# Choosing and gathering the first two turns of a mixture of experts in the mixing stage, and splitting the weights during the first expert product

## The chip, the core and the metric

One core of a Trainium2 chip runs the whole program. The metric is device microseconds of one execution. TensorE is written PE (its weight loads PEld), VectorE DVE, ScalarE ACT, GpSimd POOL, and SyncE SP.

## What is computed

Two layers over 1024 tokens of 1024 features: a token mixer (windowed attention in layer 0, a Fourier mixing in layer 1), then a mixture of 64 experts of which every token takes 8, plus one shared expert. The part that matters here is the second, cut to its core:

```python
def moe_ffn(tok, ...):
    scores = sigmoid(tok @ router_w)
    top_e = top 8 experts of the 4 best of 8 groups, by scores + bias
    wts = scores[top_e] / sum(scores[top_e]) * 2.5
    # the rows of every expert are gathered in blocks of 128
    for each block of an expert e, with rows `rows` and weights `wb`:
        xb = x_pad[rows]
        hb = silu(xb @ w_gate[e]) * (xb @ w_up[e])
        y[rows] += (hb @ w_down[e]) * wb[:, None]
    return y + (silu(tok @ s_gate) * (tok @ s_up)) @ s_down
```

## The kernel before

`moe` runs two blocks for each layer, `mix` and `experts`. A block ends when all five engines have come to its end. Then the stage's semaphores are cleared and all engines meet once more (lines 234 and 235), so that nothing of the next block starts before the last engine of the block is done.

`mix` multiplies by the output matrix, normalises, runs the shared expert in eight tiles of 128 tokens (`gate_up`, `turn_h`, `down`, with ACT's `store` and SP's write of the result to DRAM), and routes. At its end PE turns the table of places and weights (L1307, L1313), and DVE copies the places to SBUF (L1141). DVE makes a one-hot matrix for turn 0 in the 16-bit tile `hot` (L1143), which says for every slot of the turn which token stands there. It casts the weights to 16 bits into `moving[..., 3]` (L1146). PE multiplies the one-hot with three columns of `moving` (L1319), then runs `down(7)`, the last tile of the shared expert. DVE turns the product into row numbers `idx` (L1149 to L1151) and POOL gathers these rows of `u_scratch` into `xg[:, 0]` with an indirect DMA (L1022). After that DVE makes the second and third 16-bit part of the weights (L1153 to L1156). A weight in fp32 is the sum of three 16-bit parts.

`experts` works in turns of 128 rows. There are 71 in each layer, and a turn has one or two experts. In layer 0 turn 0 has the expert in ring slot 0, turn 1 that in slot 1, turn 2 those in slots 2 and 3. In layer 1 turn 1 already has two, slots 1 and 2, and turn 2 slots 2 and 3. Per turn: a one-hot (`onehot`, DVE, L1449), a product with all six columns of `moving` into `psI` (`index`, PE, L1638), the row numbers and the weights from it (`indices`, DVE, L1464 to L1472), the gather (POOL, L1415), the turned rows (`turn_rows`, PE, L1656, copied by ACT L1602 and DVE `rows` L1479), the first product (`gate_up`, PE, L1668, into `psG`), the activation (ACT L1607, DVE `hidden` L1484 to L1488), the turned result (PE L1690, ACT L1612), the second product (`down`, PE, L1702, into `psD`), the weighing (DVE L1517) and the scattered addition to `y_scratch` (POOL, L1426).

The order on each engine is written out by hand. `xg`, `hot`, `psG`, `hid` and `yo` have two buffers, so that the gather of turn 2 can be issued only when the rows of turn 0 have been turned. SP loads the experts' weights into a ring of four slots, 3 MB each (L2222 gate and up, L2225 down). Slot 0 is loaded in `mix` (L1003 to L1005). Slots 1 to 3 are loaded at the start of `experts`, after a wait for the last write of the shared expert's result (L1373). Each later load waits until the turns that used its slot are done. `table`, `overflow` and the loops with `_over` serve experts with more rows than planned, and the change does not touch them.

The beginning of PE's program in `experts` is this:

```python
                        pe.sem_inc(d_mm, 1)
                        index(0, 0)
                        index(1, 1)
                        turn_rows(0, 0, 16)
                        index(2, 0)
                        gate_up(0, 0)
                        turn_rows(1, 1, 16)
                        index(3, 1)
```

## Time and profile before

| | us |
|---|---|
| median of three runs | 2992.59 |
| lowest and highest | 2986.41, 2995.37 |
| the profiled execution | 2990.77 |
| its span, from first to last instruction | 2989.0 |
| between the two, outside the span | 1.8 |

The mean clock that TensorE was granted is 0.979 of full speed. The expert stages run from 797 to 1674 us (layer 0) and from 2050 to about 2940 us (layer 1). A row of the time line gives the start, the duration, the engine, the line, and in brackets how long the engine stood idle before it and what released it. PE instructions of one kind that follow one another are merged. Each fp32 product shows as two instructions.

### The profile page before, as it was taken

The page shows a single profiled execution, that of the slowest core. Times are in us where ns is not written, and L with a number is a line of the kernel's source. Part 1 is how long each engine was busy: PE and PEld are TensorE (multiplying, and loading weights), DVE is VectorE, ACT ScalarE, POOL GpSimd, SP SyncE. Part 2 cuts the span into 40 slices and gives each one's busy share as a digit, 9 for nine tenths or more (in the row PEclk, how much of TensorE's full clock was granted, in tenths as well). Part 3 has the DMA queues.
Part 4 walks back from the last instruction along what each step waited for, and adds up shares of the span by engine and source line. Part 5 has one row for each costly group of instructions (what it writes and reads, how often), then busy time and mean ns, then how long its engine had stood idle before and what let it go on. Part 6 is the DMA issues. An engine that isn't in the chain of part 4 may idle for free. (4 is left out here: it accounts for less than half of the span.)

```text
span 2989.0 us, 40809 instructions
## 1 busy us (share of the span) xinstructions
PE 2821.1 (94%) x15284; PEld 1368.5 (46%) x15287; DVE 1753.3 (59%) x3359; ACT 509.5 (17%) x1060; POOL 532.5 (18%) x404
## 2 busy tenths in 40 slices
PE   8998999999899999999999598997999999999994
PEld 3444666544444444444444264543444444444442
DVE  4994555466656555555555455665565555555555
ACT  1113555201110111111111240011110111111112
POOL 0000000111022222222222211101222222222212
PEclk9999999999999999999999899998999999999997
DMA  9777200201599999999999622017999999998996
GB/s 365 258 271 215 78 15 8 77 29 42 206 338 331 310 299 321 328 339 329 353 306 321 208 99 83 29 50 282 306 296 332 296 366 320 320 345 275 311 325 197
DMA packets 147086, 715.70 MB, mean 239 GB/s; under 512 B 16702, under 2 KB 21950, under 8 KB 94665
## 3 DMA queue, kind: packets, MB, share of 16 engines
q1 hardware_dynamic: 104252, 556.83, 48.6%
q0 software_dynamic: 42336, 154.16, 20.8%
q8 instruction: 124, 2.03, 0.3%
q10 hardware_dynamic: 304, 2.11, 0.2%
q14 instruction: 70, 0.57, 0.1%
HBM read 598.18 MB, written 114.84 MB: 239 GB/s over the span
## 5 line engine op out<-in xcount | busy, mean ns | idle before, releaser
L1668 PE MATMUL exG<-ring,xT 128*32 128x512 f32 (+2 forms) x2352 | 683.4, 596 | 5.2 <-DMA ring<-in_exp_w_up_dram 3.7
L1479 DVE COPY xT<-exX 128x512 f32<-128x512 f32 x146 | 101.0, 692 | 680.5 <-PE exX L1656 680.2
L1668 PEld LDWEIGHTS exG<-ring,xT 128*32 128x32 f32 (+2 forms) x2352 | 240.0, 141 | 348.0 <-issue 343.4
L1702 PE MATMUL exD<-ring,ex_hT 128*32 128x512 f32 (+2 forms) x1176 | 353.2, 603 | 1.7 <-DVE w_fnet L1517 0.8
L1612 ACT ACTIVATE ex_hT<-exH 128x256 f32<-128x256 f32 x144 | 55.2, 383 | 1454.5 <-PE exH L1690 1454.5
L1485 DVE RECIPROCAL ex_e<-ex_e 128x256 f32<-128x256 f32 x142 | 249.0, 1753 | 5.0
L1668 PE MATMUL exG<-oT,xT 128*32 128x512 f32 (+2 forms) x592 | 192.5, 597 | 1.3 <-DVE xT L1479 1.3
L1426 POOL DMA_INDIRECT y_scratch<-w_fnet,idx_out x72 | 136.1, 1891 | 299.1 <-DMA y_scratch<-w_fnet,idx_out 156.3
L1426 POOL DMA_INDIRECT y_scratch<-w_o,idx_out x72 | 132.8, 1844 | 306.3 <-DMA y_scratch<-w_o,idx_out 166.8
L1449 DVE TENSOR_TENSOR mod<-place,slots 128x1024 bf16<-128x1024 f32 (+3 forms) x196 | 174.1, 912 | 8.1 <-PEq L235 7.4
L1668 PE MATMUL exG<-w_fnet,xT 128*32 128x512 f32 (+2 forms) x608 | 172.2, 599 | 4.8 <-DMA ring<-in_exp_w_up_dram 4.8
L1702 PEld LDWEIGHTS exD<-ring,ex_hT 128*32 128x32 f32 (+2 forms) x1176 | 115.0, 140 | 126.4 <-issue 125.4
L753 DVE TENSOR_REDUCE mx<-pair 128x2 f32<-128x1280 f32 x64 | 95.5, 1492 | 125.5 <-PE pair L865 125.5
L1668 PE MATMUL exG<-w_o,xT 128*32 128x512 f32 (+2 forms) x464 | 148.2, 593 | 0.7 <-DVE xT L1479 0.7
L287 POOL TENSOR_TENSOR rstd<-var,halves 128x1 f32<-128x1 f32 x42 | 62.9, 1498 | 465.8 <-DVE var L273 465.8
L1415 POOL DMA_INDIRECT fT<-u_scratch,idx x72 | 71.2, 989 | 378.6 <-DVEq L1474 378.6
L1415 POOL DMA_INDIRECT oT<-u_scratch,idx x72 | 71.2, 989 | 366.6 <-DVEq L1474 356.2
L1668 PE MATMUL exG<-fT,xT 128*32 128x512 f32 (+2 forms) x432 | 121.5, 597 | 0.9 <-DVE xT L1479 0.9
L1223 PE MATMUL mixY<-w_fnet,fT 128*128 128x512 f32 x256 | 113.4, 601 | 6.0 <-PEq L235 4.6
L1223 PE MATMUL mixY<-w_o,oT 128*128 128x512 f32 x256 | 111.7, 594 | 3.1 <-PEq L235 1.7
L1244 PE MATMUL mixG<-sh_gate_up,u2T 128*128 128x512 f32 x256 | 112.6, 593 | 0.0
L637 PE MATMUL psQ<-w_q,uT 128*128 128x512 f32 x256 | 111.2, 592 | 0.0
(414 smaller groups left out, 4338.8 us busy)
## 6 DMA issues: line engine op xcount, KB each, us to landing
ring<-in_exp_w_gate_dram SPq DMA_DIRECT2D x64, 1024.0 KB
ring<-in_exp_w_up_dram SPq DMA_DIRECT2D x64, 1024.0 KB
ring<-in_exp_w_down_dram SPq DMA_DIRECT2D x64, 1024.0 KB
ada_w<-in_w_ada_dram SPq DMA_DIRECT2D x48, 512.0 KB, 5.6
oT<-in_exp_w_gate_dram SPq DMA_DIRECT2D x17, 1024.0 KB, 10.4
oT<-in_exp_w_up_dram SPq DMA_DIRECT2D x17, 1024.0 KB, 14.1
oT<-in_exp_w_down_dram SPq DMA_DIRECT2D x17, 1024.0 KB
fT<-in_exp_w_gate_dram SPq DMA_DIRECT2D x17, 1024.0 KB, 10.4
```

The lines of the kernel that those rows point to most:

```text
L287: pool.tensor_tensor(r["rstd"][:], r["var"][:], halves[:], ALU.pow).then_inc(r["ready"], 1)
L637: last = pe.matmul(psQ[:, c], uT[:, k], cols, start=k == 0, stop=k == KT - 1)
L753: dve.tensor_reduce(mx[:, p % 2], pair[p % 2][:, 0:2 * S].rearrange("p (a s) -> p a s", a=2), AX, ALU.max).then_inc(own, 1)
L1223: last = pe.matmul(psY[:, c], src[:, k, t * P:(t + 1) * P], w[:, k, c * 512:(c + 1) * 512], start=k == 0, stop=k == KT - 1)
L1244: last = pe.matmul(psG[:], uT[:, t % DEEP, k], wgu[:, k], start=k == 0, stop=k == KT - 1)
L1415: pool.indirect_dma_start(out=xg[:, par], out_offset=None, in_=u_dram, in_offset=bass.IndirectOffsetOnAxis(ap=idx[:, par:par + 1], axis=0) ...
L1426: pool.indirect_dma_start(out=y_dram[layer], out_offset=bass.IndirectOffsetOnAxis(ap=idx_out[:, par:par + 1], axis=0), in_=yo[:, par], in_ ...
L1449: last = dve.tensor_tensor(hot[:, par, :, at:at + n], place[:, :, r:r + 1].to_broadcast([P, NT, n]), slots[:, start:start + n].unsqueeze(1 ...
L1479: dve.tensor_copy(xT[:, par, 0:KT // 2], psX[:, 0:KT // 2]).then_inc(xT_d, 1)
L1485: link(dve.reciprocal(e[:], e[:]))
L1668: last = pe.matmul(psG[par][p:p + m], xT[:, par, k, p:p + m], ring[s % RING][:, 0:2, k * FF:(k + 1) * FF], start=k == 0, stop=k == KT - 1)
L1702: last = pe.matmul(psD[p:p + m, c], hT[:, k * P + p:k * P + p + m], ring[s % RING][:, 2, k * D + c * 512:k * D + (c + 1) * 512], start=k = ...
```

## The change

In `mix`, DVE makes the one-hots of turns 0 and 1 (two `hot` buffers), then copies the weights as they are, in fp32, to `w_rest`, a part of the `mod` tile that is no longer used. PE runs `down(7)` before the index products rather than after them, and then the three-column products of both turns. DVE makes both columns of `idx` at once. POOL waits for both and gathers both turns, into `xg[:, 0]` and `xg[:, 1]`. The 16-bit parts are no longer made here.

In `experts`, the products `index(0)` and `index(1)` are gone from the start. DVE makes the three parts after `rows(0)` (`weight_parts`, five instructions). PE multiplies the one-hots of turns 0 and 1 with all six columns inside `gate_up(0)`, ahead of the last two of its eight steps (`first_weights`, into `psD`), and DVE sums the weights from there. `onehot(2)` has to wait for this product, since it overwrites `hot[:, 0]`. `index(2)` moves behind `turn_rows(1)`, and `index(3)` into the middle of `gate_up(1)`.

The core of the diff:

```diff
@@ -1018,9 +1019,10 @@
-                        pool.wait_ge(idx_done, 1)
-                        pool.indirect_dma_start(out=xg[:, 0], out_offset=None, in_=u_dram,
-                                                in_offset=bass.IndirectOffsetOnAxis(ap=idx[:, 0:1], axis=0)).then_inc(gathered[0], 16)
+                        pool.wait_ge(idx_done, 2)
+                        for b in range(2):
+                            pool.indirect_dma_start(out=xg[:, b], out_offset=None, in_=u_dram,
+                                                    in_offset=bass.IndirectOffsetOnAxis(ap=idx[:, b:b + 1], axis=0)).then_inc(gathered[b], 16)
@@ -1139,21 +1141,18 @@
-                        for _, rr, begin, at, n in turns[0]:
-                            last = tt(hot[:, 0, :, at:at + n], place[:, :, rr:rr + 1].to_broadcast([P, NT, n]),
-                                      slots[:, begin:begin + n].unsqueeze(1).to_broadcast([P, NT, n]), ALU.is_equal)
-                        last.then_inc(hot_done, 1)
-                        dve.tensor_copy(moving[:, :, :, 3], psM[:, :, E:])
+                        for b in range(2):
+                            for _, rr, begin, at, n in turns[b]:
+                                last = tt(hot[:, b, :, at:at + n], place[:, :, rr:rr + 1].to_broadcast([P, NT, n]),
+                                          slots[:, begin:begin + n].unsqueeze(1).to_broadcast([P, NT, n]), ALU.is_equal)
+                            last.then_inc(hot_done, 1)
+                        dve.tensor_copy(w_rest, psM[:, :, E:])
...
-                        dve.wait_ge(first_mm, 1)
-                        dve.tensor_reduce(pad[:, 0:1], psG[:, 0, 0:2], AX, ALU.add)
-                        link0(ts(pad[:, 1:2], psG[:, 0, 2:3], small[:, 1:2], small[:, 0:1], ALU.mult, ALU.add))
-                        link0(tt(idx[:, 0:1], pad[:, 0:1], pad[:, 1:2], ALU.add))
-                        dve.sem_inc(idx_done, 1)
-                        link(tt(rest, psM[:, :, E:], moving[:, :, :, 3], ALU.subtract))
-                        link(dve.tensor_copy(moving[:, :, :, 4], rest))
-                        link(tt(rest, rest, moving[:, :, :, 4], ALU.subtract))
-                        link(dve.tensor_copy(moving[:, :, :, 5], rest))
+                        dve.wait_ge(idx_mm, 2)
+                        dve.tensor_reduce(pad_sum[:], psG[:, :, 0:2], AX, ALU.add)
+                        link0(ts(pad[:], psG[:, :, 2], small[:, 1:2], small[:, 0:1], ALU.mult, ALU.add))
+                        link0(tt(idx[:], pad_sum[:], pad[:], ALU.add))
+                        dve.sem_inc(idx_done, 2)
@@ -1312,18 +1311,25 @@
+                        pe.wait_ge(hT_done, NT)
+                        pe.wait_ge(yo_done, NT - 1)
+                        for k in range(FK):
+                            pe.matmul(psD[:, 0], hT[:, NT - 1, k * P:(k + 1) * P], wd[:, k, 0:512], start=k == 0, stop=k == FK - 1)
+                        for k in range(FK):
+                            last = pe.matmul(psD[:, 1], hT[:, NT - 1, k * P:(k + 1) * P], wd[:, k, 512:1024], start=k == 0, stop=k == FK - 1)
+                        last.then_inc(d_mm, 1)
...
-                        pe.wait_ge(hot_done, 1)
-                        for t in range(NT):
-                            for _, rr, p, n in pieces(turns[0]):
-                                last = pe.matmul(psG[p:p + n, 0, 0:3], hot[:, 0, t, p:p + n], moving[:, t, rr, 0:3],
-                                                 start=t == 0, stop=t == NT - 1)
-                        last.then_inc(first_mm, 1)
-                        down(7)
+                        for b in range(2):
+                            pe.wait_ge(hot_done, b + 1)
+                            for t in range(NT):
+                                for _, rr, p, n in pieces(turns[b]):
+                                    last = pe.matmul(psG[p:p + n, b, 0:3], hot[:, b, t, p:p + n], moving[:, t, rr, 0:3],
+                                                     start=t == 0, stop=t == NT - 1)
+                            last.then_inc(idx_mm, 1)
@@ -1425,7 +1431,7 @@
-                        for b in range(1, 4):
+                        for b in range(2, 4):
@@ -1444,6 +1450,8 @@
+                            if b == 2:
+                                dve.wait_ge(first_mm, 1)
@@ -1457,8 +1465,20 @@
+                        def weight_parts():
+                            link = Links(dve, parts_own)
+                            for c in range(3, 6):
+                                link(dve.tensor_copy(moving[:, :, :, c], w_rest))
+                                if c < 5:
+                                    link(dve.tensor_tensor(w_rest, w_rest, moving[:, :, :, c], ALU.subtract))
+                        def first_weights():
+                            dve.wait_ge(first_mm, 1)
+                            dve.tensor_reduce(w_all[:, 0:2], psD[:, :, 3:6], AX, ALU.add).then_inc(first_own, 1)
+                            dve.tensor_copy(idx_all[:, 0:2], idx[:])
...
-                            link = Links(dve, idx_own, 2 if isinstance(b, int) and b == 0 else b * 4 + 1)
+                            link = Links(dve, idx_own, b * 4 - 6)
@@ -1467,8 +1487,6 @@
-                            if isinstance(b, int) and b == 0:
-                                return
-                                return
                             link(dve.tensor_tensor(idx[:, par:par + 1], pad[:, 0:1], pad[:, 1:2], ALU.add))
                             assert link.n == 4
                             dve.sem_inc(idx_done, 1)
@@ -1558,17 +1576,15 @@
                             link(ts(total[:], pend[0:1, E - 1:E], 1.0, None, ALU.max))
                             dve.sem_inc(rows_done, 1)
-                        onehot(1, 1)
-                        indices(0, 0, 2)
+                        rows(0, 0, 2)
+                        weight_parts()
+                        first_weights()
                         onehot(2, 0)
-                        indices(1, 1, 2)
-                        rows(0, 0, 2)
+                        rows(1, 1, 2)
                         indices(2, 0, 2)
                         onehot(3, 1)
-                        rows(1, 1, 2)
+                        hidden(0, 0, 2)
                         indices(3, 1, 2)
-                        hidden(0, 0, 2)
                         for b in range(1, T):
                             par = b % 2
                             if b == 9:
@@ -1631,8 +1647,8 @@
-                            if b >= 1:
-                                pe.wait_ge(idx_own, 3 if b == 1 else b * 4 - 2)
+                            if b >= 3:
+                                pe.wait_ge(idx_own, b * 4 - 9)
@@ -1655,6 +1671,15 @@
+                        def first_weights():
+                            pe.wait_ge(parts_own, 5)
+                            for b in range(2):
+                                for t in range(NT):
+                                    for _, r, p, m in pieces(turns[b]):
+                                        last = pe.matmul(psD[p:p + m, b, 0:6], hot[:, b, t, p:p + m], moving[:, t, r, :],
+                                                         start=t == 0, stop=t == NT - 1)
+                            last.then_inc(first_mm, 1)
@@ -1664,6 +1689,10 @@
+                                if b == 0 and k == KT - 2:
+                                    first_weights()
+                                if b == 1 and k == KT // 2:
+                                    index(3, 1)
@@ -1694,6 +1723,8 @@
+                            if b == 0:
+                                pe.wait_ge(first_own, 1)
+                                pe.wait_ge(first_own, 1)
                             pe.wait_ge(hT_done, b + 1)
                             after(pe, y_done, b, 1)
                             for c in range(2):
@@ -1717,14 +1748,10 @@
                         pe.sem_inc(d_mm, 1)
-                        index(0, 0)
-                        index(1, 1)
                         turn_rows(0, 0, 16)
-                        index(2, 0)
                         gate_up(0, 0)
                         turn_rows(1, 1, 16)
-                        index(3, 1)
+                        index(2, 0)
                         for b in range(1, T):
                             par = b % 2
                             gate_up(b, par)
@@ -2209,8 +2236,9 @@
-                own_sems = dict(hot_done=sem("hot_done"), idx_own=sem("idx_own"), idx_done=sem("idx_done"))
-                first_mm, yo_out = sem("first_idx_mm"), [sem(f"yo_out{i}") for i in range(2)]
+                own_sems = dict(hot_done=sem("hot_done"), idx_own=sem("idx_own"), idx_done=sem("idx_done"), idx_mm=sem("idx_mm"))
+                yo_out = [sem(f"yo_out{i}") for i in range(2)]
+                w_rest = mod[:, 3 * D:3 * D + NT * EXPERTS].rearrange("p (t e) -> p t e", e=EXPERTS)
```

PE's program of layer 0 before, from the index product at the end of `mix` to the first product of turn 1. `mixG` is the bank of the index product in `mix`, `mixD` that of `down`, `exI` the index product, `exX` the turned rows, `exG` the first product.

```order
L1319 MATMUL mixG<-moving,mod 128x3 x8
L1261 MATMUL mixD<-sh_down,sh_hT 128x512 x4
L983 UNCONDITIONAL_BRANCH
L1630 UNCONDITIONAL_BRANCH
L1638 MATMUL exI<-moving,mod 128x6 x16
L1656 MATMUL exX<-ident,oT 128x128 x8
L1638 MATMUL exI<-moving,mod 32x6 x32
L1668 MATMUL exG_9<-oT,xT 128x512 x8
L1656 MATMUL exX<-ident,oT 128x128 x8
L1638 MATMUL exI<-moving,mod 128x6 x8
L1668 MATMUL exG_9<-w_o,xT 128x512 x8
L1690 MATMUL exH<-ident,ex_h 128x128 x2
```

The same stretch of PE's program in the changed kernel:

```order
L1317 MATMUL mixD<-sh_down,sh_hT 128x512 x2
L1319 MATMUL mixD<-sh_down,sh_hT 128x512 x2
L1326 MATMUL mixG<-moving,mod 128x3 x16
L984 UNCONDITIONAL_BRANCH
L1646 UNCONDITIONAL_BRANCH
L1672 MATMUL exX<-ident,oT 128x128 x8
L1697 MATMUL exG_9<-oT,xT 128x512 x6
L1680 MATMUL exD<-moving,mod 128x6 x16
L1697 MATMUL exG_9<-oT,xT 128x512 x2
L1672 MATMUL exX<-ident,oT 128x128 x8
L1654 MATMUL exI<-moving,mod 32x6 x32
L1697 MATMUL exG_9<-w_o,xT 128x512 x4
```

`down(7)` (L1317, L1319) stands ahead of the index products of two turns. In `experts` the turned rows come first, the weights' product stands inside turn 0's first product, and the index product of turn 2 behind the turned rows of turn 1.

DVE's program of layer 0 before, from the row numbers of turn 1 (L1472) to the one-hot of turn 3. POOL's gathers of turns 1 and 2 wait for the two rows `idx<-pad`.

```order
L1472 TENSOR_TENSOR idx<-pad 128x1
L1479 COPY xT<-exX 128x512
L1464 COPY pick<-exI 128x6
L1465 TENSOR_REDUCE w_all<-pick 128x1
L1466 TENSOR_REDUCE pad<-pick 128x1
L1468 TENSOR_SCALAR pad<-pick,e_small 128x1
L1469 TENSOR_TENSOR idx_all<-pad 128x1
L1472 TENSOR_TENSOR idx<-pad 128x1
L1449 TENSOR_TENSOR mod<-place,slots 128x1024
```

DVE's program in the changed kernel up to the same row numbers of turn 2. Ahead of it in `experts` stand `rows(0)` and four instructions of `weight_parts`.

```order
L1471 CAST moving<-mod 128x512
L1477 TENSOR_REDUCE w_all<-exD 128x2
L1478 CAST idx_all<-idx 128x2
L1457 TENSOR_TENSOR mod<-place,slots 128x8x32
L1457 TENSOR_TENSOR mod<-place,slots 128x8x96
L1497 COPY xT<-exX 128x512
L1484 COPY pick<-exI 128x6
L1485 TENSOR_REDUCE w_all<-pick 128x1
L1486 TENSOR_REDUCE pad<-pick 128x1
L1488 TENSOR_SCALAR pad<-pick,e_small 128x1
L1489 TENSOR_TENSOR idx_all<-pad 128x1
L1490 TENSOR_TENSOR idx<-pad 128x1
```

The row numbers of turn 2 (L1490), for which POOL's gather of turn 2 waits, now stand behind turn 1's copy of rows, which itself waits for PE to have finished the first product of turn 0.

## Rows read from the trace of the kernel before

**Rows 1.** The page: busy time and busy tenths over the whole span.
```profile
PE 2821.1 (94%) x15284; PEld 1368.5 (46%) x15287; DVE 1753.3 (59%) x3359; ACT 509.5 (17%) x1060; POOL 532.5 (18%) x404
...
DMA  9777200201599999999999622017999999998996
```

**Rows 2.** Stretches: PE, PEld, DVE, ACT, POOL busy; clock; DMA share; GB/s.
```profile
797.40:802.40 5.00, 2.76 (x56) 2.31 (x56) 4.65 (x16) 0.60 (x1) 0.63 (x2) 0.67 0.56 174
802.40:813.00 10.60, 9.85 (x32) 4.86 (x32) 2.73 (x10) 0.81 (x2) 2.25 (x2) 0.84 1.02 420
813.00:826.40 13.40, 11.92 (x42) 5.79 (x42) 9.62 (x23) 1.32 (x4) 1.87 (x2) 1.00 1.01 418
...
2064.00:2070.30 6.30, 1.46 (x18) 1.21 (x17) 4.60 (x12) 0.87 (x2) 0.94 (x1) 0.88 1.01 415
```

**Rows 3.** Waits of TensorE in layer 1's expert stage: total, times, longest.
```profile
PE exG L1668 <- DMA ring<-in_exp_w_up_dram: 8.5, 2, 4.8
```

**Rows 4.** Time line, end of the mixing stage, layer 0: start, duration, engine, line.
```profile
783.91 2.05 PE L1313 MATMUL mixY<-w_o 128*128 128x128 f32 x16 [0.94 <-ACT w_o L1212]
...
786.00 0.69 DVE L1141 COPY place<-mixY 128x512 f32<-128x512 f32 x1 [4.07 <-PE mixY L1313]
786.73 1.23 DVE L1143 TENSOR_TENSOR mod<-place,slots 128x1024 bf16<-128x1024 f32 x1
...
788.30 5.38 PE L1261 MATMUL mixD<-sh_down,sh_hT 128*128 128x512 f32 x8
...
789.78 0.16 DVE L1151 TENSOR_TENSOR idx<-pad 128x1 uint32<-128x1 f32 x1
...
790.93 1.20 POOL L1022 DMA_INDIRECT oT<-u_scratch,idx  x1 [68.51 <-DVEq L1152]
790.95 1.03 DVE L1154 CAST moving<-w_o 128x512 bf16<-128x512 f32 x1
...
794.76 0.33 SPq L1007 DMA_DIRECT2D y_scratch<-w_o  x1
```

**Rows 5.** DMA issues around the same place: KB and microseconds to landing.
```profile
y_scratch<-w_o SPq DMA_DIRECT2D x1, 512.0 KB, 3.0
```

**Rows 6.** Time line, first turns of the experts, layer 0.
```profile
797.50 0.34 PE L1638 MATMUL exI<-moving,mod 128*128 128x6 bf16 x8 [3.82 <-PEq L235]
...
798.51 0.35 SPq L2222 DMA_DIRECT2D w_o<-in_exp_w_gate_dram  x1
...
798.99 1.90 PE L1656 MATMUL exX<-ident,oT 128*128 128x128 f32 x8
...
801.65 0.69 DVE L1479 COPY xT<-exX 128x512 f32<-128x512 f32 x1
801.84 0.95 POOL L1415 DMA_INDIRECT oT<-u_scratch,idx  x1 [4.37 <-DVEq L1474]
...
802.49 8.80 PE L1668 MATMUL exG<-oT,xT 128*128 128x512 f32 x16 [1.27 <-DVE xT L1479]
...
803.56 1.86 POOL L1415 DMA_INDIRECT oT<-u_scratch,idx  x1 [0.77 <-DVEq L1474]
...
810.90 1.01 PEld L1656 LDWEIGHTS exX<-ident,oT 128*128 128x128 f32 x8 [0.45 <-DMA oT<-u_scratch,idx]
...
813.03 7.11 PE L1668 MATMUL exG<-w_o,xT 128*128 128x512 f32 x16 [0.69 <-DVE xT L1479]
```

**Rows 7.** Time line of TensorE, turn 2 of layer 0.
```profile
820.19 1.04 PE L1656 MATMUL exX<-ident,oT 128*128 128x128 f32 x8
...
826.45 7.07 PE L1668 MATMUL exG<-ring,xT 128*32 128x512 f32 x64 [1.50 <-issue]
```

**Rows 8.** Time line, turn 1 of layer 1.
```profile
2070.30 1.08 PE L1668 MATMUL exG<-w_fnet,xT 128*64 128x512 f32 x1 [4.80 <-DMA ring<-in_exp_w_up_dram]
```

**Rows 9.** Time line, a gather on quiet queues after the last turn.
```profile
1668.47 1.00 POOL L1415 DMA_INDIRECT oT<-u_scratch,idx  x1 [3.19 <-DVEq L1474]
...
1672.46 1.09 PE L1656 MATMUL exX<-ident,oT 128*128 128x128 f32 x8 [1.41 <-DMA oT<-u_scratch,idx]
```

17 lines of the change are left out of this document (9 added, 8 removed).

## The prediction

> **What bounds the kernel now.** I read the page first. TensorE is busy 94% of the span, and the DMA engines move packets nearly all the time in both expert stages [rows 1]. Then the stretches. The changed code runs in two places of some 30 us each, one per layer, where mixing ends and the experts begin. There TensorE is not the bound: from 797.40 to 802.40 it works 2.76 of 5.00 us at a granted clock of 0.67, and the DMA share, 0.56 there, is 1.01 or 1.02 as soon as the weights flow, at 415 to 420 GB/s [rows 2]. A DMA share of 1 beside a busy TensorE says that the first turns are a race of two: PE's work, and the landing of the weights for slots 1 to 3. PE loses it once in layer 0, 1.50 us before turn 2 [rows 7]. The row says "issue", but PE's other inputs are older there, so I take it for slot 3's weights. It loses once in layer 1, 4.80 us before turn 1 [rows 8]. The rest of the 8.5 us [rows 3] is a later stall, behind a load that PE itself triggers, and it moves with PE. So a shift of PE after turn 2 is a shift of the layer's end, and the sum is made of what PE gains or loses up to there.
>
> **The end of the mixing stage.** Before, PE finishes the ranked table at 783.91 + 2.05 = 785.96, waits for the one-hot, and runs `down(7)` from 788.30 for 5.38 us [rows 4]. Sixteen instructions like its eight take 7.11 us [rows 6], so eight take 3.6 at full speed, and the 2.1 us of idle cost about 1.8 us of slower clock. Now `down(7)` fills the wait: 785.96 + 3.6 = 789.6. DVE meanwhile makes two one-hots, to 786.73 + 2 x 1.23 = 789.2, and copies the weights, 0.69 like the copy of the same size, to 789.9 [rows 4]. The index products, 0.34 for eight [rows 6], end at 789.6 + 2 x 0.34 = 790.3, so PE ends this stage 3.4 us earlier, and the shared result is written some 4 us earlier. The casts of 1.03 us leave DVE [rows 4]. That saves nothing by itself, because another engine takes over as the last. DVE's three small instructions after the product need some 0.6 us (the last is 0.16), so `idx` is ready at 790.9, where it was 789.94. POOL started 0.99 us after that and took 1.20 us [rows 4]: 791.9 to 793.1. The second gather takes 0.95 us, as one that has been alone, or 1.86, as the one that came 0.8 us after another [rows 6]. I take 1.86, the row that is nearest. POOL then ends at 795.0, and at 794.1 by the other end. The last engine before was SP at 794.76 + 0.33 = 795.09 [rows 4]. The stage shrinks by 0.1 us, at most 1.0. Layer 1 has the same pattern and I give it the same. If POOL's end of block also waited until its gather has landed, the trace of before could not show it. On quiet queues that is 4.0 us from issue (1668.47 to 1672.46) [rows 9], here 793.1 + 4.0 = 797.1, so the other bound is 2.0 us lost per layer.
>
> **The start of the experts, layer 0.** All of the following is 0.1 us earlier still by the term above. PE's first instruction was at 797.50 and turning rows at 798.99, 1.90 us long [rows 6]. Without `index(0)` and `index(1)` it starts at 797.5 and ends at 799.4. DVE's copy comes at once, 0.69, to 800.1, and `gate_up(0)` 0.15 us later, at 800.3 instead of 802.49: 2.2 us gained. It takes 8.80 us [rows 6] plus the products of `first_weights`, 2 x 0.34 at most: 809.8. Its wait for the parts costs nothing: DVE needs five instructions of at most 1.03 us [rows 4], to 805.3, and PE gets there after 12 of 16 instructions, at 800.3 + 8.80 - 4 x 0.44 = 807.3. This cover is 2 us thick. Then `turn_rows(1)`, 1.04 [rows 7], which waited for its gather before (0.45) [rows 6] and doesn't now. It ends at 810.8, the copy at 811.5, `gate_up(1)` begins at 811.7 instead of 813.03, and with 7.11 and the 0.34 of `index(3)` PE stands before `turn_rows(2)` at 819.2, 1.0 us earlier than the 820.19 of [rows 7].
>
> **Where it is given back.** The gather of turn 2 was issued at 803.56 [rows 6], 16.6 us before its use. Now `indices(2)` stands behind `rows(1)`: 811.5, six small instructions of together about 1.0 us, and POOL's start 0.3 us later give 812.8. Its use is 6.4 us later. How long does a gather take? Gather 1, issued at 801.84, let PE wait until 810.90 [rows 6], that is 9.1 us, under a DMA share of 1.02 [rows 2]. The quiet one took 4.0 [rows 9]. The share at the new time is 1.01 [rows 2], so I take 9.1: it lands at 821.9, and PE idles 2.7 us. From `turn_rows(2)` to PE's readiness for `gate_up(2)` it was 826.45 - 1.50 - 820.19 = 4.8 us [rows 7]. To this comes the slow clock, 1.8 us as after the 2.1 us of idle before `down(7)`. PE is ready at 821.9 + 4.8 + 1.8 = 828.5. The weights of slot 3, landed at 826.45 before, come about 1.3 us earlier, since gather 1 (0.5 MB at 415 GB/s) [rows 2] is no longer among them. So turn 2 starts at 828.5 instead of 826.45: **2.0 us lost**. The lower bound is a gather of 4.0 us: PE is ready at 819.2 + 4.8 = 824.0, the weights decide at 825.2, and layer 0 gains 1.2 us. Layer 0 breaks even with a gather of 7.0 us if the slow clock follows the wait, 8.8 if it doesn't.
>
> The Trainium skill, "DMA: Bandwidth & Descriptors", section "Anatomy of one DMA — SWDGE (gpsimd) path", fits a gather of this kind by 2.0 us plus the bytes at 436 GB/s. That is 3.2 us here, by an estimate from that page, and speaks against my 9.1. The wait in rows 6 contradicts it under load. By the page the sum of layer 0 would be the lower bound's.
>
> **Layer 1.** PE stood at turn 1 for slot 2's weights until 2070.30 [rows 8]. Do these land earlier? Their issue hardly moves: the first load came 0.75 us after the shared result had landed, 794.76 + 3.0 = 797.8 [rows 4, 5, 6], which is 0.3 us behind the stage's start anyway. I count nothing. But two gathers of 0.5 MB no longer share the engines with them, the first being done and the second not yet issued. At 415 GB/s [rows 2] these are 1.26 us each, 2.5 together. Less 0.34 for `index(3)`, **2.2 us gained**. The bounds: nothing gained (the gathers only used gaps, -0.3), or the weights no longer decide and PE's readiness does, 4.80 + 1.3 - 0.3 = 5.8 us. The gather of turn 2 has 9.7 us of `gate_up(1)` more to land here, since PE waits for weights first. After turn 2 nothing differs.
>
> **Sum.** +2.0 (layer 0), -2.2 (layer 1), -0.1 twice: -0.4 us on the profiled execution's 2990.77, that is 2990.4. That execution lies 1.8 us below the median of the runs shown, so I forecast 2992 for a median. The bounds: +2.0 + 0.3 + 4.0 = 6.3 above, and -1.2 - 5.8 - 2.0 = -9.0 below.
>
> **Rivals.** (1) The gather of turn 2 is in time (landing within 6.4 us). For it: the quiet 4.0 us. Against: the wait of rows 6. Layer 0 then gives -1.2: -3.6 in all, 2989. This is also what the page's fit gives. (2) POOL closes the mixing stage late, because the block's end waits for the gathers' data. Price 2.0 us per layer, from the point at which POOL's end passes 795.09: -0.4 + 0.2 + 4.0 = +3.8, 2996, slower than before. For it: POOL was never last in the trace, so nothing excludes it. Against: nothing in the rows shows an engine waiting for its own DMA. (3) Slot 2's weights in layer 1 come so early that PE decides: 3.6 us more than my sum, 2989, and 2984 with every other term at its lower bound. (4) The change moves work without a net effect (weights land as before, the gather in time, both small): within 1 us of before.
>
> **Chances.** Forecast 0.45, rival 1 0.25, rival 2 0.15, rival 3 0.10, rival 4 0.05. A measurement of this kernel can tell about 0.3% from no change, 9 us. Only the far end of rival 3 goes beyond it (0.04), and rival 2 only where the slow clock or a stall of the weights comes on top (0.03). The range takes in rivals 1 to 3 and some 4 us of spread in the runs: 2984 to 2998.
>
> **What would show it.** Before the experts' start: `down(7)` at 3.6 us right after the ranked table, two gathers on POOL, the second 1.86 us, and the next stage beginning 2.2 us after its end. In layer 0: `gate_up(0)` at 800.3 without a gap before its last four instructions, `gate_up(1)` at 811.7, and a wait of about 2.7 us for the gather at turn 2 with slow instructions behind it. In layer 1: a wait for weights at turn 1 that ends near 2067.8. I am wrong if DVE's parts or one-hots make PE wait, if the weights' landing doesn't follow the gathers, or if anything differs after turn 3.

## The result: 0.22% slower, and the profile after

| | before | changed |
|---|---|---|
| median, us (16 runs each) | 2995.18 | 3001.12 |
| lowest and highest | 2986.41, 2999.26 | 2997.84, 3011.24 |
| ratio of the two, 95% interval | | 1.0022 [1.0015, 1.0028] |
| span of the profiled execution | 2989.0 | 3000.7 |

The changed kernel is slower by 0.22%, which is 4.5 to 8.4 us, 6.6 in the middle. I had forecast -0.4 us and a range of 2984 to 2998. The interval lies below the 0.3% that I had called the limit of a measurement, but it does not hold 1.

To compare the traces I measure from t0, the start of the ranked-table product at the end of mixing. In layer 0 it is 783.91 before [rows 4] and 787.59 after. Nothing up to there was changed. Those 3.7 us are spread between executions, as the second profile of the kernel before shows further on. First the end of the changed kernel's mixing stage in layer 0, from the time line (start, duration, engine, line, and in brackets the idle time before and what ended it):

```profile
787.59 2.05 PE L1312 MATMUL mixY<-w_o 128*128 128x128 f32 x16 [0.94 <-ACT w_o L1211]
...
789.48 1.88 PE L1317 MATMUL mixD<-sh_down,sh_hT 128*128 128x512 f32 x4
...
790.40 2.36 DVE L1146 TENSOR_TENSOR mod<-place,slots 128x1024 bf16<-128x1024 f32 x2
...
791.20 1.88 PE L1319 MATMUL mixD<-sh_down,sh_hT 128*128 128x512 f32 x4
...
792.91 0.54 PE L1326 MATMUL mixG<-moving,mod 128*128 128x3 bf16 x16
...
793.88 0.16 DVE L1154 TENSOR_TENSOR idx<-pad_sum,pad 128x2 uint32<-128x2 f32 x1
794.16 0.33 SPq L1008 DMA_DIRECT2D y_scratch<-w_o  x1
795.03 1.20 POOL L1024 DMA_INDIRECT oT<-u_scratch,idx  x1 [68.94 <-DVEq L1155]
796.54 0.95 POOL L1024 DMA_INDIRECT oT<-u_scratch,idx  x1 [0.30 <-issue]
803.88 0.34 SPq L1378 DMA_DIRECT2D ex_caps<-in_caps_dram  x1
...
804.09 1.94 PE L1672 MATMUL exX<-ident,oT 128*128 128x128 f32 x8 [10.63 <-PEq L235]
```

`down(7)` fills PE's wait at full speed, 1.88 and 1.88 us for its halves, and PE is done at 793.45, 3.9 us sooner than before counted from t0 (forecast 3.4). `idx` is there at 794.04, t0 + 6.5 (forecast 7.0). The second gather's row takes 0.95 us and not the 1.86 that I took, so POOL's visible end is 797.49, t0 + 9.9, where I had put 11.1, or 10.2 with the shorter row. But the next block begins at 803.88, t0 + 16.3, where before it began at t0 + 13.4. It is 6.4 us behind POOL's last row, and I had said 2.2.

The rows of the barrier say why. Each engine ends the block with a DRAIN. These are the DRAIN rows of the kernel before in layer 0 (count, duration in ns min/median/max, first and last start):

```profile
L983 PEldq DRAIN  x1: 5453/5453/5453, 788.3 to 788.3; - x1
L983 POOLq DRAIN  x1: 5719/5719/5719, 790.7 to 790.7; - x1
...
L983 SPq DRAIN  x1: 135/135/135, 795.1 to 795.1; - x1
```

And those of the changed kernel:

```profile
L984 SPq DRAIN  x1: 135/135/135, 794.5 to 794.5; - x1
L984 POOLq DRAIN  x1: 7737/7737/7737, 795.3 to 795.3; - x1
```

POOL's DRAIN begins before its last gather row has ended, and lasted 5.7 us before and 7.7 us after. It ended at 796.4 and 803.0, and the next block's first instruction followed 0.9 us later in both. SP's DRAIN takes 0.1 us. So before the change, too, it was POOL that ended the stage, at 796.4, while SP, with its last issue at 795.09, came in only 1.3 us ahead of that.

What POOL's DRAIN covers can be read from the DMA queues. In the changed kernel, from the end of SP's DRAIN to the block's start (794.68 to 803.88; packets, MB, share of the 16 engines' time):

```profile
q1 hardware_dynamic: 320, 1.70, 49.2%
q0 software_dynamic: 288, 1.05, 28.9%
```

q0 carries POOL's two gathers, q1 SP's transfers. SP had passed its DRAIN with 1.7 MB of its own transfers still to move, and both gathers moved entirely inside POOL's DRAIN. In the kernel before, from the end of POOL's DRAIN to the block's start (796.41 to 797.3), q0 is empty and q1 still moves:

```profile
q1 hardware_dynamic: 65, 0.20, 57.4%
```

In all ten profiles with a gather in mixing, in both layers, the last packet of q0 ends 0.4 to 0.6 us before POOL's DRAIN does.

The first turns of layer 0 after:

```profile
806.90 7.12 PE L1697 MATMUL exG<-oT,xT 128*128 128x512 f32 x12 [0.88 <-DVE xT L1497]
...
813.86 0.54 PE L1680 MATMUL exD<-moving,mod 128*128 128x6 bf16 x16
...
816.07 1.04 PE L1672 MATMUL exX<-ident,oT 128*128 128x128 f32 x8
...
817.98 3.67 PE L1697 MATMUL exG<-w_o,xT 128*128 128x512 f32 x8 [0.58 <-DVE xT L1497]
...
819.05 1.87 POOL L1421 DMA_INDIRECT oT<-u_scratch,idx  x1 [15.00 <-DVEq L1492]
```

```profile
829.73 1.09 PE L1672 MATMUL exX<-ident,oT 128*128 128x128 f32 x8 [4.14 <-DMA oT<-u_scratch,idx]
...
830.87 5.38 PE L1733 MATMUL exD<-oT,ex_hT 128*128 128x512 f32 x8
836.17 7.07 PE L1697 MATMUL exG<-ring,xT 128*32 128x512 f32 x64
```

From the block's start to `gate_up(0)` it is 3.0 us where it was 5.2. `first_weights` (L1680) stands in the product without a gap. DVE's last part ended at 811.56, 2.3 us before PE needed it. PE then waits 4.14 us for gather 2, issued at 819.05 and landed by 829.73, 10.7 us later, and the second product behind that wait takes 5.38 us instead of 3.68. The granted clock says why (stretch, busy time of PE, PEld, DVE, ACT, POOL, clock, DMA share, GB/s):

```profile
818.00:821.60 3.60, 3.60 (x13) 1.59 (x14) 3.35 (x8) 0.01 (x1) 1.87 (x1) 1.00 1.00 414
830.90:836.20 5.30, 5.30 (x17) 2.05 (x14) 4.52 (x12) 0.83 (x2) 0.94 (x1) 0.68 1.02 414
836.20:843.00 6.80, 6.80 (x65) 1.95 (x64) 2.48 (x3) 0.00 (x0) 2.08 (x1) 1.00 1.02 407
```

0.68 over that product, where it was 1.00 before the wait and is 1.00 again behind it. Turn 2's `gate_up` begins at t0 + 48.6. Before it was t0 + 42.5 [rows 7].

Layer 1, the first weight load in `experts` and turn 1's first product:

```profile
2067.07 0.34 SPq L2250 DMA_DIRECT2D w_fnet<-in_exp_w_gate_dram  x1
...
2082.27 0.62 PE L1697 MATMUL exG<-w_fnet,xT 128*64 128x512 f32 x1 [2.16 <-DMA ring<-in_exp_w_up_dram]
```

15.2 us lie between them, where 18.8 us lay before (18.4 in the second profile of the kernel before): the weights of slot 2 do come faster. But the load starts 3.4 us later, since the block does, and turn 1 begins at t0 + 33.7, where it was t0 + 33.9 [rows 8]. Turn 2 begins at t0 + 48.4, before at t0 + 48.5.

So at turn 2 layer 0 has lost 6.0 us and layer 1 gained 0.2. From turn 2 to turn 9 of layer 0 the distance between the two traces stays within 0.01 us. Then it shrinks once, to 4.5 us at turn 10, and stays there up to turn 68. Between these turns PE waits for a one-hot that stands behind `overflow` in DVE's program, 2.3 us before and 2.5 us after. Each time line row is followed here by the 4 us behind the wait (busy times, then clock, DMA share, GB/s), first before, then changed:

```profile
921.08 0.35 PE L1638 MATMUL exI<-moving,mod 128*128 128x6 bf16 x8 [2.34 <-DVE mod L1449]
...
921.10:925.10 4.00, 4.00 (x29) 1.19 (x33) 3.68 (x10) 0.00 (x0) 0.98 (x1) 0.61 0.68 170
```

```profile
930.98 0.35 PE L1654 MATMUL exI<-moving,mod 128*128 128x6 bf16 x8 [2.51 <-DVE mod L1457]
...
930.98:934.98 4.00, 4.00 (x42) 1.34 (x44) 3.68 (x10) 0.00 (x0) 0.98 (x1) 1.00 0.73 166
```

The granted clock was 0.61 behind the wait in one trace and 1.00 in the other. Why it fell in one and not in the other is open.

### The profile page after: what moved, and what is told of

It reads as the page before. It is cut to its first block and busy times, and to the rows that moved or that the text cites. A ratio compares the mean times of both kernels' runs of the same rounds, so it can differ in the third digit from the quotient of the medians.

```text
span 3000.7 us, 40835 instructions
## 1 busy us (share of the span) xinstructions
PE 2823.0 (94%) x15308; PEld 1368.4 (46%) x15311; DVE 1751.2 (58%) x3343; ACT 510.1 (17%) x1060; POOL 530.2 (18%) x404
## 3 DMA queue, kind: packets, MB, share of 16 engines
q1 hardware_dynamic: 104252, 556.83, 48.4%
## 6 DMA issues: line engine op xcount, KB each, us to landing
ring<-in_exp_w_gate_dram SPq DMA_DIRECT2D x64, 1024.0 KB, 10.2
```

## The experiments

Three theories of the stage's end: (A) it waits until POOL's own gathers have landed, (B) it comes a fixed time after the last row of any engine, as I had forecast, (C) it waits for SP's loads as well. And one question behind it: how much of layer 0's loss is the wait for gather 2.

Offsets from t0 in us, layer 0 / layer 1. "Block" is SP's first instruction in `experts`. "Turn 4" and "turn 20" are `gate_up(4)` and `gate_up(20)`. PE repeats its pattern between them but for the wait at `overflow`, and in layer 1 some waits of turns 15 and 16. b_two_gathers and a_store7_late were executed once, for their profile, and have no ratio. h_hot3 stands in its own paragraph alone.

| kernel | block | gate_up(0) | gate_up(1) | gate_up(2) | turn 4 | turn 20 | ratio to before, 95% interval |
|---|---|---|---|---|---|---|---|
| before | 13.4 / 14.0 | 18.6 / 19.2 | 29.1 / 33.9 | 42.5 / 48.5 | 66.6 / 72.5 | 261.9 / 271.2 | |
| before_again | 13.3 / 13.5 | 18.5 / 18.8 | 29.5 / 33.0 | 42.6 / 46.6 | 66.6 / 70.6 | 261.9 / 270.7 | 0.9998 [0.9990, 1.0007] |
| changed | 16.3 / 17.4 | 19.3 / 20.4 | 30.4 / 33.7 | 48.6 / 48.4 | 72.6 / 72.3 | 266.4 / 270.5 | 1.0022 [1.0015, 1.0028] |
| b_down_first | 15.2 / 15.3 | 20.4 / 20.5 | 31.6 / 34.2 | 43.5 / 46.2 | 67.6 / 70.2 | 261.2 / 270.1 | 1.0013 [1.0002, 1.0024] |
| b_two_gathers | 16.8 / 18.2 | 22.0 / 23.4 | 32.5 / 37.1 | 46.2 / 50.8 | 70.2 / 74.7 | 265.6 / 276.4 | |
| a_gather1_late | 15.6 / 15.6 | 18.6 / 18.6 | 30.0 / 33.3 | 48.6 / 47.8 | 72.6 / 71.8 | 266.3 / 270.3 | 1.0013 [1.0001, 1.0026] |
| a_store7_late | 15.5 / 15.6 | 18.5 / 18.6 | 29.8 / 35.3 | 48.3 / 49.2 | 72.4 / 73.2 | 266.0 / 273.4 | |
| a_down0_late | 15.1 / 15.4 | 18.2 / 18.4 | 29.7 / 34.5 | 48.3 / 48.9 | 72.4 / 72.8 | 266.0 / 270.7 | 1.0041 [1.0025, 1.0056] |
| a_gathers_late | 8.0 / 7.9 | 18.3 / 17.4 | 29.8 / 30.5 | 48.4 / 44.9 | 72.4 / 68.9 | 266.0 / 267.2 | 1.0006 [0.9993, 1.0019] |
| h_hot3_mended | 16.3 / 17.0 | 19.3 / 20.1 | 31.8 / 36.2 | 44.0 / 51.4 | 68.0 / 75.4 | 261.6 / 276.2 | 1.0028 [1.0017, 1.0039] |
| h_late | 8.0 / 7.9 | 18.2 / 18.2 | 29.8 / 32.9 | 41.9 / 46.9 | 65.9 / 70.9 | 261.4 / 271.3 | 1.0010 [1.0000, 1.0019] |
| h_late_down0 | 8.0 / 7.9 | 19.7 / 16.4 | 32.1 / 32.4 | 44.3 / 47.8 | 68.3 / 71.7 | 261.9 / 270.2 | 1.0016 [1.0007, 1.0025] |
| h_layered | 8.0 / 7.9 | 18.4 / 17.4 | 30.3 / 30.3 | 42.4 / 44.1 | 66.5 / 68.1 | 260.1 / 269.4 | 0.9997 [0.9988, 1.0005] |

**How far two executions of one kernel differ.** before_again is the kernel before, unchanged.

> The kernel before, unchanged, profiled and timed once more. All other kernels of this study reach the end of layer 0's mixing 2 to 5 us later than the first profile of before (its ranked table starts at 783.91), though their programs are the same up to there. Theory: this is spread, periods of the lower clock that fall here in one execution and there in another; the new profile has its ranked table at 785 to 789 and its time is 1.000 of before within 0.1%. Rival: the edits move something outside the changed stretches, then the new profile repeats 783.9 and before's own offsets within 0.5 us.

```profile
788.58 2.05 PE L1313 MATMUL mixY<-w_o 128*128 128x128 f32 x16 [0.94 <-ACT w_o L1212]
...
795.60 1.20 POOL L1022 DMA_INDIRECT oT<-u_scratch,idx  x1 [68.51 <-DVEq L1152]
...
801.92 0.34 SPq L1372 DMA_DIRECT2D ex_caps<-in_caps_dram  x1
```

t0 is at 788.58, 4.7 us later than in the first profile of the same kernel, with the ratio at 0.9998. Layer 0 repeats the first profile's offsets within 0.4 us and its turn 2 within 0.1. In layer 1 turn 2 comes 2.0 us earlier than in the first profile. From layer 0's turn 5 to layer 1's t0 it took 1177.8 us, before 1174.0. The first profile of before was a quick one, by some 5 us in code that no edit touches, and the granted clock goes the same way: 1.00 over the 200 us ahead of t0, and 0.98 in before_again. So offsets are read from t0. In layer 1 I take 2 us as their spread, and the ratios carry whatever the rest of the program adds. Against before_again the changed kernel's layer 1 did not gain 0.2 us at turn 2 but lost 1.8.

**What ends the mixing stage.** In the kernel before, `down(7)` moved and nothing else:

```diff
+                        down(7)
                         pe.wait_ge(iota_done, 1)
                         pe.wait_ge(hot_done, 1)
...
                         last.then_inc(first_mm, 1)
-                        down(7)
```

> The kernel before with one edit: down(7) stands ahead of the index product at the end of mixing, as in the changed kernel; still one gather in mixing. t0 is the start of the ranked-table product on PE (L1313). Before, the next block starts at t0 + 13.4 us in layer 0 and t0 + 14.0 in layer 1. Theory A: POOL cannot leave the block before its gather's data have landed (its DRAIN row), and the gather shares the DMA engines with slot 0's 3 MB of weights, so the bytes decide and the block starts at t0 + 13.0 to 14.5 in both layers, time within 2 us of before. Theory B (that of my prediction): the block ends 2.2 us after the last visible end of an engine. SP now ends at t0 + 7, POOL's row at t0 + 8.2, so the block starts at t0 + 10.4 in both layers and the kernel is 6 us faster.

```profile
L983 POOLq DRAIN  x1: 7328/7328/7328, 793.8 to 793.8; - x1
...
oT<-u_scratch,idx POOLq DMA_INDIRECT x1, 7.0
```

The second row is the gather's issue with its time to landing: issued at 794.06, it had landed at 801.1, and the DRAIN ended at 801.1. The block starts at t0 + 15.2 and 15.3. Theory B, on which my prediction stood, said 10.4 and falls. A was right that nothing is gained. But the start is also 1.8 and 1.3 us later than before, and later than the 14.5 that I had given A at most. The time, 1.0013, is 3.9 us above before (0.6 to 7.2) where I had said within 2. The gather is issued only 0.2 us later, yet the DRAIN lasts 7.3 us instead of 5.7. What changed beside it is that tile 7's store (0.5 MB to DRAM) now goes out ahead of the gather, at t0 + 6.6 instead of behind it at t0 + 10.9. The gather's first packet moved at t0 + 11.3, where it moved at t0 + 9.7 before. Both gathers taken out of the stage:

```diff
-                        pool.wait_ge(idx_done, 2)
-                        for b in range(2):
-                            pool.indirect_dma_start(out=xg[:, b], out_offset=None, in_=u_dram,
-                                                    in_offset=bass.IndirectOffsetOnAxis(ap=idx[:, b:b + 1], axis=0)).then_inc(gathered[b], 16)
...
-                        for b in range(2, 4):
+                        for b in range(0, 4):
                             gather(b, b % 2, 2)
```

> The changed kernel with both gathers issued at POOL's start in experts, not in mixing. Theory A (DRAIN waits for POOL's own gathers): POOL's DRAIN at the end of mixing is short and the block starts about 2.2 us after SP's last issue, at t0 + 9 instead of t0 + 16.3 and 17.4; PE then waits for gather 0, issued at t0 + 9.5 and landing 4 to 6 us later, and begins turning rows at about t0 + 14 instead of 16.5. Theory C (DRAIN waits for all DMA traffic, slot 0's weights too): the start stays at t0 + 12 or later. Time by A: 3 to 6 us below the changed kernel; by C: within 2 us of it.

```profile
795.90 0.14 POOL L1409 IOTA ex_ks<- 128x8 f32 x1 [69.46 <-POOLq L235]
796.71 1.20 POOL L1417 DMA_INDIRECT oT<-u_scratch,idx  x1 [0.67 <-issue]
798.22 0.95 POOL L1417 DMA_INDIRECT oT<-u_scratch,idx  x1 [0.30 <-issue]
818.76 1.86 POOL L1417 DMA_INDIRECT oT<-u_scratch,idx  x1 [19.59 <-DVEq L1488]
```

```profile
803.41 1.97 PE L1668 MATMUL exX<-ident,oT 128*128 128x128 f32 x8 [9.61 <-DMA oT<-u_scratch,idx]
...
829.05 1.97 PE L1668 MATMUL exX<-ident,oT 128*128 128x128 f32 x8 [3.75 <-DMA oT<-u_scratch,idx]
```

The block starts at t0 + 8.0 and 7.9, 8.3 and 9.4 us sooner than in the changed kernel, with slot 0's weights still on their way. POOL's DRAIN, now with no gather ahead of it, is a row of 0.04 us at 731.4. That rules out theory C and, with the queues above, shows A: POOL's DRAIN waits for POOL's own transfers, not for SP's. Most of it is not gained, since PE now waits for gather 0, issued at 796.71 and landed by 803.41, 6.7 us later (5.5 in layer 1), where I had expected 4 to 6. The ratio is 1.0006, whose interval holds 1. By the two ratios this is 4.8 us below the changed kernel, inside the 3 to 6 of theory A. The opposite test is one transfer more in the kernel before:

```diff
                         pool.indirect_dma_start(out=xg[:, 0], out_offset=None, in_=u_dram,
                                                 in_offset=bass.IndirectOffsetOnAxis(ap=idx[:, 0:1], axis=0)).then_inc(gathered[0], 16)
+                        pool.indirect_dma_start(out=mod[:, 3 * D:4 * D], out_offset=None, in_=u_dram,
+                                                in_offset=bass.IndirectOffsetOnAxis(ap=idx[:, 0:1], axis=0)).then_inc(spare, 16)
```

> The kernel before with turn 0's gather issued twice in mixing, the second into a part of SBUF that nothing reads, on a semaphore that nobody waits for. Nothing waits for this transfer but, by theory A, POOL's DRAIN at the block's end. Theory A: the block starts 0.7 to 2 us later, at t0 + 14.1 to 15.4 in layer 0 (13.4) and 14.7 to 16 in layer 1 (14.0). Rival: a DRAIN does not cover a transfer nobody waits for, then the start moves by less than 0.3 us.

```profile
L984 POOLq DRAIN  x1: 8689/8689/8689, 794.3 to 794.3; - x1
...
mod<-u_scratch,idx POOLq DMA_INDIRECT x1, 7.3
```

The DRAIN covers a transfer that nobody waits for: issued at 795.61, it had landed at 802.9, the DRAIN ended at 803.0, and the start moves by 3.5 us in layer 0 and 4.2 in layer 1. That is about twice the 0.7 to 2 us that I had said. With slot 0's weights beside them, the packets of the two gathers took 5.8 and 7.0 us from the first to the last, those of the one gather before 2.4 and 2.7. The remaining three each take one transfer out of the changed kernel's stage, to divide its 2.9 and 3.4 us.

In a_gather1_late:

```diff
                         pool.wait_ge(idx_done, 2)
-                        for b in range(2):
+                        for b in range(1):
                             pool.indirect_dma_start(out=xg[:, b], out_offset=None, in_=u_dram,
...
-                        for b in range(2, 4):
+                        for b in range(1, 4):
                             gather(b, b % 2, 2)
```

> The changed kernel with only turn 0's gather in mixing; turn 1's is the first thing POOL issues in experts. Its row numbers are still made in mixing. Theory A: half the gathered bytes before the block's end, so it starts at t0 + 13.5 to 14.5 instead of 16.3 and 17.4; gather 1 lands within 9 us, before PE has finished turn 0's first product (12 us), so PE does not wait for it. Layer 0 still waits about 4 us for gather 2. 4 to 5 us below the changed kernel, 1 to 3 above the kernel before. Theory B: the second gather's 1 us is all that is saved, 2 us for both layers.

In a_store7_late:

```diff
                             sp.wait_ge(yo_done, t + 1)
-                            sp.dma_start(y_dram[layer].rearrange("(r j) d -> r j d", j=2)[t * P:(t + 1) * P, 0], yo[t % 2]).then_inc(yo_out[t % 2], 16)
+                            if t < NT - 1:
+                                sp.dma_start(y_dram[layer].rearrange("(r j) d -> r j d", j=2)[t * P:(t + 1) * P, 0], yo[t % 2]).then_inc(yo_out[t % 2], 16)
...
+                        sp.dma_start(y_dram[layer].rearrange("(r j) d -> r j d", j=2)[(NT - 1) * P:NT * P, 0], last_yo).then_inc(yo_out[1], 16)
                         sp.wait_ge(yo_out[1], 16 * (NT // 2))
```

> The changed kernel with the store of the shared expert's last tile (0.5 MB to DRAM) issued at the start of experts, not in mixing. With down(7) moved ahead this store goes out before the gathers, at t0 + 6.6, where it went out at t0 + 10.9 before, behind the gather. Theory: that order is what delays the gathers' landing beyond the extra gather, so POOL's DRAIN ends 1 to 2 us sooner, the block starts at t0 + 14.5 to 15.3 in layer 0 (16.3) and 15.4 to 16.4 in layer 1 (17.4). Rival: the store does not matter, starts unchanged within 0.5 us.

In a_down0_late:

```diff
                                 load_in(sp, ex, 0)
-                                load_down(sp, ex, 0)
...
                         for s in range(1, RING):
+                            if s == 2:
+                                load_down(sp, expert(sp, ORDER[layer][0]), 0)
```

> The changed kernel with one transfer moved: the third MB of slot 0 (the second product's weights) is loaded in experts, after slot 1, not in mixing. Both gathers stay in mixing. Theory A (POOL's DRAIN lasts until its gathers have landed, and these share the engines with slot 0's weights): 1 MB less at 400 GB/s, the block starts 2 to 2.6 us sooner, at t0 + 13.7 to 14.3 in layer 0 and 14.8 to 15.4 in layer 1. Rival: the gathers' own latency decides, not the bytes beside them: the start stays at t0 + 16.3 and 17.4.

One gather less starts the block 0.7 and 1.8 us sooner than in the changed kernel, the store taken out 0.8 and 1.8, 1 MB of slot 0's weights taken out 1.2 and 2.0. Each has the sign that theory A gives it. In layer 0 all three miss the size they were given: A by bytes alone said 1.8 to 2.8 us for the gather, 2 to 2.6 for the MB, and 1 at least for the store. In layer 1 the store and the MB reach it, and the gather, for which 2.9 us at least were expected, does not. a_gather1_late's time is 2.7 us below the changed kernel's by the two ratios, where I had put 4 to 5. a_store7_late's later turns lose what the start gains: SP waits for the store before it loads slot 1, 4.9 us behind the block's start in layer 0 instead of 1.1. So the stage ends when POOL's gathers have landed, and these land later with every transfer beside them, but how much later is not simply the bytes. a_down0_late's ratio, 1.0041, is worse than the changed kernel's, while its offsets at turns 4 and 20 are the same within 0.5 us. The stretches I compared do not explain that.

**Layer 0's wait for gather 2.** A third one-hot buffer in the free part of `mod`. DVE fills it at the end of mixing, PE makes the row numbers from it right after turn 0's rows, and its weights come with those of turns 0 and 1:

```diff
+                hot2 = mod[:, 3 * D + NT * EXPERTS:4 * D].bitcast(BF16).rearrange("p (t c) -> p t c", t=NT)
...
                         rows(0, 0, 2)
+                        indices(2, 0, 2)
                         weight_parts()
                         first_weights()
-                        onehot(2, 0)
-                        rows(1, 1, 2)
-                        indices(2, 0, 2)
                         onehot(3, 1)
+                        rows(1, 1, 2)
...
                         turn_rows(0, 0, 16)
+                        index_two()
                         gate_up(0, 0)
                         turn_rows(1, 1, 16)
-                        index(2, 0)
```

> The changed kernel with a third one-hot buffer: the one-hot of turn 2 is made by DVE at the end of mixing, its row numbers come from a three-column product right after turn 0's rows, and its weights from the product inside the first expert product. Gather 2 is issued some 3.5 us after the block's start instead of 15. Theory: layer 0's 4.14 us wait for gather 2 and the slow down(0) behind it (5.38 instead of 3.6) go, the weights of slot 3 may take a part of that back; 3 to 6 us below the changed kernel, nothing gained in layer 1 (0.3 us of waiting there). Rival: the wait for slot 3's weights takes its place whole, since gather 2's bytes now compete with them, and the gain is under 2 us.

In this first form DVE keeps the row numbers of turns 0 and 1 only after turn 2's have overwritten one of them. A turn's results are then added to wrong rows, and layer 1 makes 75 scattered additions where before makes 72, so its time of 3072.73 says nothing of the change. Its layer 0 up to turn 4 is the same work: `gate_up(2)` at t0 + 43.2. The mended form:

```diff
                         rows(0, 0, 2)
+                        dve.tensor_copy(idx_all[:, 0:2], idx[:])
                         indices(2, 0, 2)
...
-                            dve.tensor_copy(idx_all[:, 0:2], idx[:])
```

> The changed kernel with a third one-hot buffer, as in h_hot3, with the row numbers of turns 0 and 1 copied before turn 2's overwrite them. Theory: gather 2 is issued near t0 + 20 instead of t0 + 31.5, PE does not wait for it, and gate_up(2) of layer 0 starts near t0 + 43.2 instead of t0 + 48.6; about 5 us below the changed kernel, and 1 to 2 above the kernel before, whose block starts 3 us sooner. Rival: most of layer 0's loss is the later start of the block, then gate_up(2) stays at t0 + 45 or later.

Time line of PE at turn 2 of layer 0, and PE's waits there from 790 to 850:

```profile
825.09 1.04 PE L1687 MATMUL exX<-ident,oT 128*128 128x128 f32 x8
...
826.17 3.68 PE L1752 MATMUL exD<-oT,ex_hT 128*128 128x512 f32 x8
...
829.78 5.79 PE L1716 MATMUL exG<-ring,xT 128*32 128x512 f32 x52
```

```profile
PE exX L1687 <- PEq L235: 10.6, 1, 10.6
PE exG L1716 <- DVE xT L1504: 1.4, 2, 0.9
```

No wait for gather 2 is left, the second product takes 3.68 us, and turn 2 begins at t0 + 44.0 instead of 48.6: 4.6 us back, 0.8 less than in h_hot3's profile. So of the 6.0 us that layer 0 had lost at turn 2, an earlier gather 2 brings back 4.6. The rival (45 or later) falls. But the kernel as a whole got no faster, 1.0028: in layer 1 turn 2 moved to t0 + 51.4, 3.0 us later than in the changed kernel. There gather 2's 0.5 MB, issued at t0 + 21 instead of 33, now runs ahead of the weights that turn 1 waits for. I had expected nothing there. The pair of h_late and h_layered below tests this cause.

**Putting it together.** h_late is h_hot3_mended with turn 2's one-hot and both gathers moved to the start of `experts`:

```diff
-                        pool.wait_ge(idx_done, 2)
-                        for b in range(2):
-                            pool.indirect_dma_start(out=xg[:, b], out_offset=None, in_=u_dram,
...
-                        for b in range(2, 4):
+                        for b in range(0, 4):
```

> The changed kernel with a third one-hot buffer (its one-hot made at the start of experts) and with both gathers issued at the start of experts. Theory: no DRAIN of POOL, the next block starts at t0 + 8; gathers near t0 + 8.8 and 10.3, PE turns rows at t0 + 15 in both layers, gather 2 in time; gate_up(2) at t0 + 41 to 42.5 in layer 0 (before 42.5, changed 48.6) and near t0 + 45 in layer 1 (before 48.5, changed 48.4). 4 us below the kernel before and 10 below the changed one. Rival: the earlier weight loads and three gathers at once delay gather 0 beyond t0 + 16 and all is lost again: within 2 us of before.

h_late_down0 moves a part of slot 0's weights as well:

```diff
-                                load_down(sp, ex, 0)
...
+                            if s == 2:
+                                load_down(sp, expert(sp, ORDER[layer][0]), 0)
```

> As h_late, and slot 0's second-product weights are loaded in experts behind slot 1. Theory: gather 0 no longer queues beside the third MB, so it lands 1 to 2.5 us sooner and PE turns rows at t0 + 13 to 14; 1 to 2 us per layer below h_late if PE and not the weights of slots 2 and 3 set turn 2. Rival: the MB is only moved among the loads that turn 1 of layer 1 and turn 2 of layer 0 wait for, then gate_up(2) is where h_late has it, or 2.5 us later in layer 1.

h_late's offsets at turn 2 are 41.9, where I had put them, and 46.9, 2 us later than I had put it in layer 1. Its time is not where I had put it: 1.0010, not 4 us below before but about 3 above (interval 0 to 6). A part of this is lost behind turn 4. In layer 1 h_late is 1.6 us ahead of the kernel before at turn 4 and 0.1 behind it at turn 20. The difference arises at the wait at `overflow`, where the clock behind it was 0.65 in h_late and 1.00 in the first profile of before (0.70 in before_again). The other 3 us are not explained by the offsets. h_late_down0 moves the third MB too and gains nothing: gather 0 lands 1.8 us sooner in layer 1, 1.5 later in layer 0. The last version keeps gather 2 early only in the layer that needs it:

```diff
                         dve.tensor_copy(idx_all[:, 0:2], idx[:])
-                        indices(2, 0, 2)
+                        if layer == 0:
+                            indices(2, 0, 2)
...
                         rows(1, 1, 2)
+                        if layer == 1:
+                            indices(2, 0, 2)
```

> As h_late (three one-hot buffers, both gathers at the start of experts), but in layer 1 turn 2's row numbers and gather come only after turn 1's rows, as in the changed kernel. In layer 0 PE is not waiting for weights before turn 2 and needs gather 2 early; in layer 1 PE waits for slot 2's weights before turn 1, and gather 2's 0.5 MB ahead of them delays them. Theory: layer 0 as in h_late, gate_up(2) near t0 + 42, layer 1 as in a_gathers_late, near t0 + 45 instead of h_late's 46.9 and before's 48.5; 4 us below before, about 2 below h_late. Rival: the landing times spread by 2 us from run to run, and the order of the gathers decides nothing: layer 1 at t0 + 46 to 48.

PE's waits for transfers around the start of layer 1's experts, h_late and then h_layered:

```profile
PE exX L1683 <- DMA fT<-u_scratch,idx: 9.3, 1, 9.3
PE exG L1712 <- DMA ring<-in_exp_w_up_dram: 3.6, 1, 3.6
```

```profile
PE exX L1686 <- DMA fT<-u_scratch,idx: 9.7, 2, 8.5
PE exG L1715 <- DMA ring<-in_exp_w_up_dram: 1.8, 1, 1.8
```

The wait for slot 2's weights falls from 3.6 to 1.8 us, a wait of 1.2 us for gather 2 is back, and turn 2 begins at t0 + 44.1, the earliest of all. With 0.9997 [0.9988, 1.0005] this kernel takes back all that the change had cost, and cannot be told from the kernel before. By the offsets at turn 20 it should be about 3 us faster (1.8 in layer 0, 1.8 or 1.3 in layer 1, by the profile of before that is taken). The runs show 0.9 us, and their interval ends at 3.6. In every edited kernel with a ratio the time, taken at the middle of its interval, is longer than its offsets at turn 20 say, by 0.4 us (a_gather1_late) to 8.7 (a_down0_late). With one profile of each, where these microseconds stand remains open.

## Why the prediction was wrong, step by step

**The end of the mixing stage: wrong, and the main fault.** I read the last visible end of any engine (SP, 795.09) and added what lay behind it. The step that failed is the sentence "the last engine before was SP". It was POOL, whose DRAIN row ran to 796.4. That SP stood only 1.3 us ahead of this made the wrong reading look right. I forecast -0.1 us per layer and measured +2.9 and +3.4. What the runs showed in its place is my rival 2, the block's end waiting for the gathers' data, at a chance of 0.15 and with 2.0 us per layer as its price, from a quiet gather's 4.0 us. I wrote that no row showed an engine waiting for its own DMA, and that the trace of before could not show it. The DRAIN rows and the queues of the trace of before show just that, and I had not asked for them. The price was low because the gathers don't run quiet here (6.7 us in a_gathers_late). The store of tile 7, which now goes ahead of them, has a part in it too (b_down_first: 1.8 and 1.3 us without any second gather, a_store7_late: 0.8 and 1.8 us back without the store).

**The start of the experts: right.** From the block's start `gate_up(0)` gained 2.2 us, as forecast, and `gate_up(1)` 1.6, forecast 1.3. The cover held: DVE's parts were done 2.3 us early, forecast 2.0.

**Gather 2 in layer 0: the mechanism right, the size short.** I forecast a landing of 9.1 us, a wait of 2.7 and 1.8 us of slower clock. The landing took 10.7 (10.3 and 10.1 in a_gathers_late and a_gather1_late), the wait 4.14, and the slow product cost 1.7. From the block's start to turn 2 layer 0 lost 3.1 us, forecast 2.0. The Trainium skill ("DMA: Bandwidth & Descriptors", section "Anatomy of one DMA — SWDGE (gpsimd) path") fits a DMA of this kind by 2.0 us plus its bytes at 436 GB/s, by an estimate from that page 3.2 us for this size. All three landings contradict it for this place, and so does the 6.7 us of gather 0.

**Layer 1: the mechanism right, the size too small.** With fewer gathers ahead of them, slot 2's weights took 15.2 us from the first load instead of 18.8: 3.6 us against the first profile of before and 3.2 against the second, where I had 2.5. The late start of the block ate it. h_late and h_layered differ only in when gather 2 of layer 1 is issued (t0 + 19.2 and t0 + 30.5), and turn 1 starts at t0 + 32.9 and 30.3.

**After turn 2: not as forecast.** I had written that nothing differs there, and that I would be wrong if anything differed after turn 3. In layer 0 the two traces differ at `overflow`, where 1.5 us of the loss disappear. Nothing of the 1.5 us was in the sum.

**The sum.** -0.1 x 2, +2.0 and -2.2 gave -0.4. With the measured terms up to turn 2 it is +2.9 and +3.4 for the stage, +3.1 and -3.6 behind it: +5.9 in the two profiles (without rounding). At turn 20 it is +4.5 and -0.6, together +3.9, against 6.6 (4.5 to 8.4) by the ratio. So the agreement of 5.9 with 6.6 is in part luck, and some 2.7 us of the slowdown are not found in these stretches. The range was also set on a median of three runs, 2992.59, which was 2.6 us below that of sixteen. That alone did not carry the result over 2998: 3001.12 - 2.6 is 2998.5. Rival 2 with its right price would have come near: 2992.2 (the forecast's 2992.59 - 0.4) + 0.2 + 6.3 = 2998.7, and with layer 0's full loss behind the block, 1.1 more, 2999.8.
